# Mixture-of-experts output: per-expert scatter through TensorE, or rows stored in DRAM and fetched back at the end

## The reference, cut to what matters

```
def moe_ffn(h, router_w, w1, w3, w2):
    logits = (h @ router_w).astype(jnp.float32)
    vals, idx = lax.top_k(logits, TOP_K_EXPERTS)          # 2 of 8
    probs = jax.nn.softmax(vals, axis=-1)
    gate = jnp.sum(jax.nn.one_hot(idx, N_EXPERTS, ...) * probs[..., None], axis=-2)
    out = jnp.zeros_like(h)
    for e in range(N_EXPERTS):
        out = out + gate[..., e:e + 1] * swiglu(h, w1[e], w3[e], w2[e])
    return out        # added to x; swiglu(h, a, b, c) = (silu(h @ a) * (h @ b)) @ c
```

## Time and profile before

| quantity | value |
|---|---|
| three timed runs | 1776.13, 1776.93, 1778.08 us |
| median | 1776.93 us |
| profiled execution, first to last instruction (span) | 1775.2 us |
| profiled execution's own time | not listed apart from its span; the median lies 1.7 us above the span |
| busy: PE, DVE, ACT, POOL | 1705.0, 1390.7, 1064.8, 404.7 us |
| mean granted TensorE clock | 0.983 of full |
| moved by DMA | 475.76 MB, mean 268 GB/s |

### The profile page before, as it was taken

The page is one execution under the profiler, slowest core; times in us unless marked ns, Lnnn a source line. Parts: engine busy times, 40 slices in busy tenths (PEclk is TensorE's granted clock), DMA queues, the critical chain, the costliest instruction groups (busy, mean ns, idle before and its releaser), DMA issues.

```text
span 1775.2 us, 24479 instructions
## 1 busy us (share of the span) xinstructions
PE 1705.0 (96%) x9030; PEld 1442.4 (81%) x9030; DVE 1390.7 (78%) x1172; ACT 1064.8 (60%) x874; POOL 404.7 (23%) x492
## 2 busy tenths in 40 slices
PE   7899998999979999979999999999999999999998
PEld 5887877999868888767888888888888888888886
DVE  6989565455459886558898898898898988988987
ACT  5344445444344444447777777777777777777775
POOL 8979400998024342000000000000000000000000
PEclk9999999999989999979999999999999999999999
DMA  8433365556443443539999999999999999999995
GB/s 313 143 107 119 121 202 179 183 183 207 147 144 120 134 163 127 186 106 335 384 354 364 376 357 374 366 344 385 364 342 391 355 363 377 356 376 370 350 372 183
DMA packets 210841, 475.76 MB, mean 268 GB/s; under 512 B 7729, under 2 KB 32433, under 8 KB 210529
## 3 DMA queue, kind: packets, MB, share of 16 engines
q1 hardware_dynamic: 207456, 463.34, 73.5%
q0 software_dynamic: 2896, 11.01, 1.7%
q10 hardware_dynamic: 432, 0.65, 0.1%
HBM read 471.30 MB, written 3.67 MB: 268 GB/s over the span
## 4 chain that ended last, share of the span: by engine, by line
PE 81%; DVE 13%; issue 2%; ACT 1%; POOL 1%; DMA 0%; DVEq 0%; ACTq 0%; POOLq 0%
PE ps L619 24%; PE ps L621 23%; PE ps L620 23%; DVE w_lo L264 5%; PE ps L643 1%; PE ps L1073 1%; PE ps L644 1%; PE ps L645 1%; DVE x_tok L2085 1%; PE ps L742 1%; PE ps L685 1%; PE ps L767 1%; ACT w_hi L259 1%; PE ps L769 1%; POOL trig L294 1%
## 5 line engine op out<-in xcount | busy, mean ns | idle before, releaser
L264 DVE TENSOR_TENSOR w_lo<-raw,w_hi 128x2048 fp32r<-128x2048 f32 (+1 forms) x439 | 1011.7, 2313 | 246.3 <-ACT w_hi L259 244.8
L259 ACT ACTIVATE w_hi<-raw 128x2048 fp32r<-128x2048 f32 (+1 forms) x439 | 839.6, 1915 | 412.6 <-PE ps L621 393.1
L619 PE MATMUL ps<-w_hi,xg_hi 128*128 128x512 f32 x896 | 357.7, 399 | 3.3 <-issue 1.4
L621 PE MATMUL ps<-w_hi,xg_lo 128*128 128x512 f32 x896 | 350.3, 391 | 0.0
L620 PE MATMUL ps<-w_lo,xg_hi 128*128 128x512 f32 x896 | 349.8, 390 | 0.0
L619 PE MATMUL ps<-w_hi,hT_hi 128*128 128x256 f32 (+2 forms) x672 | 228.9, 341 | 2.2 <-DVE hT_lo L1604 2.2
L620 PE MATMUL ps<-w_lo,hT_hi 128*128 128x256 f32 (+2 forms) x672 | 225.0, 335 | 0.0
L621 PE MATMUL ps<-w_hi,hT_lo 128*128 128x256 f32 (+2 forms) x672 | 224.6, 334 | 0.0
L619 PE MATMUL ps<-w_hi,hidT_hi 128*128 128x512 f32 x536 | 209.6, 391 | 2.8 <-DVE hidT_lo L1926 2.8
L621 PE MATMUL ps<-w_hi,hidT_lo 128*128 128x512 f32 x536 | 208.8, 390 | 0.0
L620 PE MATMUL ps<-w_lo,hidT_hi 128*128 128x512 f32 x536 | 208.7, 389 | 0.0
(11 more groups left out here) (331 smaller groups left out, 2018.8 us busy)
## 6 DMA issues: line engine op xcount, KB each, us to landing
raw<-moe_w SPq DMA_DIRECT2D x336, 1024.0 KB, 7.2
raw<-w_in SPq DMA_DIRECT2D x44, 1024.0 KB, 5.4
raw<-ffn_w SPq DMA_DIRECT2D x33, 1024.0 KB, 5.3
raw<-w_o SPq DMA_DIRECT2D x8, 1024.0 KB, 5.0
raw<-w_out_a SPq DMA_DIRECT2D x4, 1024.0 KB, 5.0
raw<-w_out_c SPq DMA_DIRECT2D x4, 1024.0 KB, 5.0
raw<-w_out_b SPq DMA_DIRECT2D x4, 1024.0 KB, 5.0
raw<-w_in SPq DMA_DIRECT2D x4, 904.0 KB, 7.1
```

Source lines behind the costliest of these rows:

```text
L259: act.activation(w_hi[:, n % SPLIT, 0:width], raw[:, n % RAW, 0:width], ACT.Copy).then_inc(hi_done, 1)
L264: dve.tensor_tensor(w_lo[:, n % SPLIT, 0:width], raw[:, n % RAW, 0:width], w_hi[:, n % SPLIT, 0:width].bitcast(F32), ALU.subtract).then_in ...
L619: pe.matmul(dst, x_hi, hi, start=first, stop=False, skip_group_check=True)
L621: return pe.matmul(dst, x_lo, hi, start=False, stop=last, skip_group_check=True)
```

## The change

For experts 0 to 6 there is no `y_hi`/`y_lo`, no `turn_pick`, no `scatter` and no `add_to_x`. ACT copies the result from PSUM to a tile `y_sb` in one instruction of 128x1024, and POOL stores it to a DRAM tensor `y_rows` (512 KB per expert). POOL also computes once, in `places`, for every token the two rows of `y_rows` that belong to it and their gates (34 small instructions). In the eighth expert POOL fetches these rows with four indirect DMAs of 512 KB into `y_back`, and DVE adds them in two steps (`add_rows`, two instructions of 128x1024 each), one before and one after the last ordinary stripe. The eighth expert's own result still takes the old way. A token that sits in only one of experts 0 to 6 has a gate of zero for the other row.

The core of the diff:

```
 def expert(e, last):                                  # PE
-    pe.wait_ge(S["acc_done"], 4 * (e0 + e) + 1)
+    if rnd == 0:
+        pe.wait_ge(S["y_taken"], e + 1)
     down(n0 + 8, i + 1, turns, first=True)
     turn_hidden(i + 1)
-    turn_pick(e)
+    if last or rnd > 0:
+        turn_pick(e)
...
-    scatter(e, last)
+    if last or rnd > 0:
+        scatter(e, last)

 def expert(e, last):                                  # ACT, at the end of experts 0 to 6
+    if rnd == 0 and not last:
+        act.wait_ge(S["rows_stored"], 16 * e + 16)
+        act.activation(y_sb[:, :], banks(2, 2), ACT.Copy).then_inc(S["y_taken"], 1)

 def add_rows(k):                                      # DVE, new
+    dve.wait_ge(S["y_loaded"], 16 * 2 * BLOCKS)
...
+    for b in range(BLOCKS):
+        dve.scalar_tensor_tensor(x_tok[:, b, :], y_back[:, b, k, :], gate_of_choice[:, k, b:b + 1],
+                                 x_tok[:, b, :], ALU.mult, ALU.add).then_inc(S["acc_done"], 1)

 def expert(e, last):                                  # DVE
     if not last:
-        dve.wait_ge(S["pickT_ps"], e_at)
         pick_slots(value(dve, e + 1), rnd)
...
+    if last and rnd == 0:
+        add_rows(0)
     stripe(i, t, turns + t - 1)                       # t = 6
+    if last and rnd == 0:
+        add_rows(1)
     lo(n0 + 10, turns + t - 1)
...
-    add_to_x(e)                                       # and y(e): now only in a second round

 # POOL
+    def store_y(e):
+        pool.wait_ge(S["y_taken"], e + 2)
+        pool.dma_start(y_rows[e * P:(e + 1) * P, :], y_sb[:, :]).then_inc(S["rows_stored"], 16)
...
+    places()
     for e in range(1, EXPERTS):
+        if e >= 2:
+            store_y(e - 2)
         pool.wait_ge(S["token_done"], e)
         pool.wait_ge(S["gather_ps"], 2 * e)
         pool.indirect_dma_start(xg_tok ...)
+    store_y(EXPERTS - 2)
+    pool.wait_ge(S["rows_stored"], 16 * EXPERTS)
+    for k in range(2):
+        for b in range(BLOCKS):
+            pool.indirect_dma_start(y_back[:, b, k, :], None, y_rows,
+                                    bass.IndirectOffsetOnAxis(row_of_choice[:, k, b:b + 1], 0))...
```

More of the change, by code:

```diff
@@ L1503, in expert @@
                     split_hi(act, n0 + 11, turns)
-                    act.wait_ge(S["pickT_ps"], e0 + e + 1)
-                    act.activation(flat(pickT[:, :, :]), ps[:, 5, 0:2 * P], ACT.Copy).then_inc(S["pickT_done"], 1)
+                    if last or rnd > 0:
+                        act.wait_ge(S["pickT_ps"], 1 if rnd == 0 else 1 + e + 1)
+                        act.activation(flat(pickT[:, :, :]), ps[:, 5, 0:2 * P], ACT.Copy)\
+                           .then_inc(S["pickT_done"], 1)
                     with act.Fori(2, MOE_STRIPES - 1) as t:
@@ L1528, in expert @@
                         act.wait_ge(used, n0 + 8 + 6 * (turns + t))
-                    for half in range(2):
+                    if rnd == 0 and not last:
+                        act.wait_ge(S["rows_stored"], 16 * e + 16)
+                        act.activation(y_sb[:, :], banks(2, 2), ACT.Copy).then_inc(S["y_taken"], 1)
+                    for half in range(2 if last or rnd > 0 else 0):
                         if last and half == 1:
@@ L2262, in norm_and_rope, with places @@
                 rotary(0, 10, "rope_done")
+            def places():
+                rows, held, count, so_far, which, part = (place[:, k] for k in range(6))
+                last = EXPERTS - 1
+                for b in range(BLOCKS):
+                    own.step(pool.tensor_scalar(rows[:, b, :], slot_id[:, 0, 0:EXPERTS], float(P), 1.0, ALU.mult,
+                                                ALU.add))
+                own.step(pool.tensor_scalar(held, slot_of[:, :, 0:EXPERTS], float(P), None, ALU.is_lt))
+                own.join()
+                own.step(pool.tensor_tensor(rows, rows, slot_of[:, :, 0:EXPERTS], ALU.add))
+                own.then(pool.tensor_tensor(held, held, rt[:, 7], ALU.mult))
+                own.then(pool.memset(held[:, :, last:EXPERTS], 0.0))
+                own.step(pool.tensor_copy(count[:, :, 0:1], held[:, :, 0:1]))
+                own.then(pool.tensor_tensor(count[:, :, 1:8], held[:, :, 1:8], held[:, :, 0:7], ALU.add))
+                own.step(pool.tensor_copy(so_far[:, :, 0:2], count[:, :, 0:2]))
+                own.then(pool.tensor_tensor(so_far[:, :, 2:8], count[:, :, 2:8], count[:, :, 0:6], ALU.add))
+                own.step(pool.tensor_copy(count[:, :, 0:4], so_far[:, :, 0:4]))
+                own.then(pool.tensor_tensor(count[:, :, 4:8], so_far[:, :, 4:8], so_far[:, :, 0:4], ALU.add))
+                for k in range(2):
+                    own.then(pool.tensor_scalar(which, count, float(k + 1), None, ALU.is_equal))
+                    own.then(pool.tensor_tensor(which, which, held, ALU.mult))
+                    for per_expert, per_choice in ((rows, row_f[:, k, :]), (gate_of[:, :, :], gate_of_choice[:, k, :])):
+                        own.then(pool.tensor_tensor(part, which, per_expert, ALU.mult))
+                        own.then(pool.tensor_tensor(part[:, :, 0:4], part[:, :, 0:4], part[:, :, 4:8], ALU.add))
+                        own.then(pool.tensor_tensor(part[:, :, 0:2], part[:, :, 0:2], part[:, :, 2:4], ALU.add))
+                        own.then(pool.tensor_tensor(per_choice, part[:, :, 0], part[:, :, 1], ALU.add))
+                own.then(pool.tensor_scalar(row_f[:, :, :], row_f[:, :, :], -1.0, 0.0, ALU.add, ALU.max))
+                pool.tensor_copy(row_of_choice[:, :, :], row_f[:, :, :]).then_inc(S["places_made"], 1)
+                pool.wait_ge(S["places_made"], 1)
```

56 lines of the change are left out of this document (41 added, 15 removed).

## The result

The changed kernel takes 1763.96 us (median of 4 runs, 1763.59 to 1765.13) against 1777.51 us of the kernel before on the same chip (4 runs, 1776.13 to 1778.48): a ratio of 0.9925, interval 0.9914 to 0.9937. The gain is three quarters of a percent and well clear of the spread. The profiled execution has a span of 1761.8 us instead of 1775.2. The prediction was 1766.7 us, 10.2 less than before; in the spans it became 13.4 less, in the medians 13.55.

A forecast was written before the change was run, and what follows sets the result against it. The prediction took PE to set the pace of the expert stage. Its terms -12.4 (seven experts), +1.4 (additions) and +0.8 (burst) summed to -10.2 us, from 1776.9 to 1766.7 us, range 1759.5 to 1774.

The forecast's parts named there:

- The turn: Between experts, without the scatter, PE's last-to-first matmul distance falls from 2.40 to 1.64 us: 0.76 us gained, seven times.
- rival 2: Full removed work gained if `hid` were ready in time at the turn: 2.83 us per expert, 1759 us; chance 6%.
- The two stalls: PE's stalls behind the turn and a stripe later, from DVE's additions and `turn_pick` wait, go: 0.78 us per expert.
- the ring of three buffers: ACT and DVE refill a freed buffer while PE works 5.45 us on two others; holds with 1.1 us to spare.
- Pick transposes: PE no longer transposes `pick` in experts 0 to 6: 0.23 us gained per expert.
- The additions: Eighth expert: four DVE additions take 5.1 us, idle time covers 3.76, the rest delays PE's last `down`: +1.4 us.
- The burst: Eighth expert's first 25 us: one store and four 512 KB fetches use up the loads' lead: +0.8 us, bounds 0 and 4.3.
- two prices: Cost to the loads of one 512 KB fetch: 1.8 us from landing times, or 1.3 us by bytes at 406 GB/s.
- Rival 3: The burst stalls PE in the eighth expert by 4.3 us and the additions cost 3: 1772 us; chance 14%.
- rival 1: Experts 0 to 6: DMA side already the bound, decided by a sustained ceiling below 368 GB/s: 1788 us; chance 7%.
- Rival 4: Stores eat part of the loads' lead in every expert, PE stalls about 1.5 us in each: 1777 us; chance 5%.
- the main term: Experts 0 to 6: turn, stalls and pick transposes together save 1.77 us per expert, seven times, -12.4 us.

The follow-up runs named there:

- e3: Changed kernel plus eight unused 128x128 by 512 matmuls on PE where the scatter stood, in experts 0 to 6: 1768.97 us, ratio 0.9952.
- e4: Changed kernel with the second `up` before the `down` at the turn, and ACT's copy to `y_sb` a stripe later: 1757.14 us, ratio 0.9882.
- e1: Changed kernel with the pick transposes, ACT's `pickT` copy and DVE's wait put back in experts 0 to 6: 1769.46 us, ratio 0.9962.
- e2: Changed kernel plus four 128x512 DVE additions at the end of experts 0 to 6, into a tile nobody reads: 1773.56 us, ratio 0.9982.
- e8: e4's order with the eighth expert's fetches spread one per stripe and its additions spread 1 + 1 + 2: 1756.71 us, ratio 0.9885.
- e6: Changed kernel without the `y_rows` stores and the four fetches, `y_back` filled with zeros: 1764.23 us, ratio 0.9927.
- e10: Changed kernel with six further 512 KB stores per expert, to DRAM rows nobody reads: 1771.9 us, ratio 0.9968.
- e7: Changed kernel with two more 512 KB fetches behind the four in the eighth expert, into an idle tile: 1767.0 us, ratio 0.9939.
- e9: Changed kernel with three further 512 KB stores per expert, to DRAM rows nobody reads: 1764.49 us, ratio 0.9935.

## Why the prediction came out right, and where it did not

**The turn, 0.76 us: right, shown.** The wait for `hid` is there with its 0.84 us, last-to-first is 1.64, and e3 gives 0.73 from the other side. The full 1.82 of rival 2 is refuted by it. The prediction noted that nothing in the changed program makes `hid` earlier; e4 does it by an exchange of two calls, and gains 1.09 more per expert.

**The two stalls, 0.78 us: gone, as predicted, and slightly larger.** The one behind the turn was 0.39 in the stretch read, 0.48 in the eighth expert, and 0.44 by the first period. The one behind `pick` is e1's 0.41. The period fell by 1.90 and not 1.77. Counted from one stripe's transposes to the next, the stripe behind the turn became 0.46 us shorter (reckoned 0.39), the second 0.62 (reckoned 0.62) and the last, with the turn, 0.81 (reckoned 0.76). Why the turn saves 0.05 more this way is not traced. Where I expected the ring of three buffers to hold with 1.1 us to spare, it holds.

**A reading that was right only in this combination.** The prediction added turn and stall as separate terms. e2 shows that they are one: with the additions kept, the turn's gain is lost again in the stall. Since both went, the sum of separate terms was correct. On a change that drops the scatter alone, the same reading would have failed by 0.8 us per expert.

**Pick transposes, 0.23: right** (0.22 in e1).

**The additions, +1.4: mis-sized, measured 0.84**, and for the greater part in another place. The prediction let them fall on PE's last `down`: only 0.14 fell there, as `hidT_lo` came 1.41 us after the start of its transposes, where it was 1.27. The first pair stalls PE one stripe before, which the prediction did not look for. By its sum this pair alone, 2.6 us against 3.76 of idle time, would have been free, and it cost 0.70: the split right behind it comes late, and idle time further on does not help that one. That the total is smaller than 1.4 all the same lies in the lengths. In a row without gaps DVE starts the next instruction about 0.08 us before the end of the one in front: a pair takes 2.39 us from start to start (1729.78 to 1732.17), the four 4.79 and not 5.1. For the same reason each of the four places where DVE idled in the earlier trace rows was worth some 0.08 us more than the idle time printed. With 0.19 us of idle time left over after, 4.79 - 3.76 - 0.3 + 0.2 = 0.9, an estimate. e8 shows the same four instructions at no cost when spread.

**The burst, +0.8: mis-sized, measured 0** (e6). The way to a stall was right, as landing rose to 12.8 us and one load had no lead left, but it ended at ACT. Of the prediction's two prices the one by bytes, 1.3 us, was near (1.39 for a store by e10), and the 1.8 read from one pair of loads was not a price per fetch: e7 lost 2.1 for two. The lead alone did not decide: ACT waited 0.28 us for a load and nothing of it reached PE, so the ring behind ACT holds some reserve as well; how much, no run measures. Rival 3 did not happen here. It did in e10, where the lead was small when the burst began (the eighth expert 1.7 us longer), and in e4, where PE is faster and the burst later (0.9 us longer). The +0.8 itself was picked between 0.5 and 4.3 without a working of its own, so that it lay near 0 is in part luck.

**Rivals 1 and 4 are refuted.** The share of 0.99 was no ceiling; e9 adds 11 GB/s to the 378 and nothing moves, and e10 finds the ceiling at 398, 30 above the 368 from which rival 1 would have decided. Rival 4 falls with e6: without any store the period is the same 120.11 us. "DMA: Bandwidth & Descriptors" of the Trainium skill gives 358 GB/s per core under Specifications; the traces contradict it as a limit for this lone core, with 389 GB/s at no cost. "HBM Reference" of the Trainium skill, Specifications (TRN2), tells of some 425 GB/s for a core that streams alone; no run here held more than 398 over a whole period, or more than 406 over 16 us.

**The terms together:** predicted -12.4, +1.4, +0.8; measured -13.3 (periods 12.80 and the last turn's stall 0.48), +0.84 and 0. The rest, -1.0, is the start of the stage (-0.75) and the time behind the last `down` (-0.23), which vary from run to run. So the 3.2 us of error in the spans are some 0.9 in the main term, 0.6 and 0.8 in the two costs, and 1.0 that the change did not make. All four made the kernel faster than predicted, so no error hid another; the sum stayed within the range because the main term was right to 7%.

## What to carry to other kernels

Before counting removed instructions as gain, find what the next instruction really waits for, and look for a place in the same trace where that wait already stands without cover; here it gave the turn to a hundredth of a microsecond. Where two engines wait for each other in turn, a gain on one and a stall on the other can be the same time: here the one was worth nothing without the other. Work added to an engine with idle time is weighed at the place where it is put in, by what waits right behind it, and by the distance from start to start. A transfer burst is priced by its bytes over the rate measured under load, and then against the lead of the loads at the moment it starts.

## What the runs showed of the hardware beyond that

- The DMA side of this core carried 389 GB/s of loads and stores with no effect on a PE-bound loop (e9), and no more than 398 GB/s over whole periods when more was asked (e10), with a "DMA share" of 1.04. Over 16 us at a time it reached 405 (e4, 1651 to 1667 us). A share of 0.99 or 1.02 is therefore no sign of saturation.
- A weight load that landed 12.8 us after its issue, instead of 7.6, did no harm with a ring that asks early. One load without any lead at ACT did not reach PE (the changed kernel); ten in a row did (e4).
- DVE instructions in an unbroken row start 2.20 us apart where a split is listed with 2.28, and 1.20 where an addition of 128x1024 is listed with 1.28: the listed lengths overlap by 0.08 us.
- A pause of 1.2 us between matmul starts at each turn left the granted clock at 1.00 in the stretches above, its 2.4 GHz level; only the first matmul behind it is slow to start (0.31 us to the next instead of 0.23), as it was before the change.
